# A hybrid decoder step: first loads of the merge issued during the attention, scores weighed in the projection's tail, gates stored by ACT

## The reference

```
h = rmsnorm(x)
qA kA vA | qB kB vB | gate_a gate_b = h @ w_in               # 46 tiles of 128 columns
branch A (8 heads x 64), stick-breaking attention; samples read a paged cache of K and V:
    z = q.k / sqrt(64) + b_h
    a = exp(log_sigmoid(z) + sum over later keys of log_sigmoid(-z));   oA = a @ v
branch B (3 groups x 4 heads x 64), sliding windows (128,1) (512,4) (2048,16) with ALiBi:
    the 3 groups' outputs are mixed by their softmax denominators -> oB
x = x + (sigmoid(gate_a) * (oA @ w_br_a) + sigmoid(gate_b) * (oB @ w_br_b)) @ w_o
x = x + moe(rmsnorm(x))     # top 1 of 4 groups, then top 2 of 8 experts; 32 experts, hidden 512
y = rmsnorm(x)
outputs also: new K and V of the prompt, and the sample caches of branch B shifted by one row
```

## Time and profile before

| what | value |
|---|---|
| median of 3 runs | 1505.83 us (1504.05 to 1510.8) |
| the profiled execution's own time, and its span | 1503.77 us, 1501.9 us |
| PE busy in the span | 1195.9 us, 80% |
| DVE, ACT, POOL busy | 583.7, 248.9, 276.1 us |
| moved by DMA | 455.45 MB, mean 303 GB/s |
| `weigh_a` block | 396 to 421 us |
| `attend` block | 421 to 684 us |
| first `wa` load issued, first `wa` matmul | 684.07 us, 694.43 us |

### The profile page before, as it was taken

One profiled execution on the slowest core, in us unless ns is written; L12 is line 12 of the kernel. 1 busy time (PEld: TensorE's weight loads), 2 busy tenths in 40 slices (PEclk: granted clock), 3 DMA queues, 4 the chain that ended last, 5 costly groups with the idle time before them and its releaser, 6 DMA issues. The chain is left out here.

```text
span 1501.9 us, 14581 instructions
## 1 busy us (share of the span) xinstructions
PE 1195.9 (80%) x5502; PEld 687.0 (46%) x5502; DVE 583.7 (39%) x761; ACT 248.9 (17%) x400; POOL 276.1 (18%) x205
## 2 busy tenths in 40 slices
PE   4999999889469999896379983698888878877870
PEld 3878888678324454444244543233233323323320
DVE  2199999993344444532232225111111111111115
ACT  2121011100234433430000210111101011010112
POOL 2045444542002322220000000111001000100010
PEclk9999999989769999997679995799999999998995
DMA  6789999998137888987912106599999999999964
GB/s 205 294 317 386 390 372 394 399 377 293 43 101 292 316 362 322 381 326 292 314 38 84 43 25 270 195 406 411 405 408 406 408 403 409 408 397 406 410 238 185
DMA packets 102756, 455.45 MB, mean 303 GB/s; under 512 B 13581, under 2 KB 45629, under 8 KB 55365
## 3 DMA queue, kind: packets, MB, share of 16 engines
q1 hardware_dynamic: 71477, 304.12, 51.8%
q0 software_dynamic: 24176, 144.13, 24.7%
q10 hardware_dynamic: 7056, 6.57, 1.4%
HBM read 442.10 MB, written 65.44 MB: 338 GB/s over the span
## 5 line engine op out<-in xcount | busy, mean ns | idle before, releaser
L457 PE MATMUL proj_ps<-hT,w_slots 128*128 128x260 f32 x1472 | 334.8, 388 | 14.2 <-ACT stage L480 12.0
L457 PEld LDWEIGHTS proj_ps<-hT,w_slots 128*128 128x128 f32 x1472 | 281.4, 193 | 65.5 <-issue 21.0
L1759 PE MATMUL ex_gp<-raw,ex_xT 128*64 128x512 f32 x1024 | 232.5, 602 | 21.8 <-DMA raw<-in_w_up_e 14.0
L1773 PE MATMUL ex_yp<-raw,ex_hmT 128*64 128x512 f32 x512 | 141.2, 702 | 66.6 <-DMA raw<-in_w_down_e 66.1
L209 POOL DMA_INDIRECT ring<-in_cache_k_a,run_sb x64 | 137.5, 2149 | 194.5 <-DVE scores L515 167.5
L508 DVE TENSOR_TENSOR ring<-ring,q_rep 128x2048 f32<-128x2048 f32 x64 | 145.9, 2281 | 42.8 <-ACT q_rep L499 41.9
L515 DVE TENSOR_REDUCE scores<-ring 128x32 f32<-128x2048 f32 x64 | 145.8, 2279 | 0.0
L1759 PEld LDWEIGHTS ex_gp<-raw,ex_xT 128*64 128x64 f32 x1024 | 71.2, 138 | 159.3 <-issue 124.4
L1714 DVE TENSOR_TENSOR ex_hm<-ex_sg,ex_gp 64x512 f32<-64x512 f32 x32 | 21.7, 679 | 268.5 <-ACT ex_sg L1694 268.5
L209 POOL DMA_INDIRECT ring<-in_cache_v_a,run_sb x64 | 73.2, 1144 | 258.3 <-PE at_vp L726 242.5
L1773 PEld LDWEIGHTS ex_yp<-raw,ex_hmT 128*64 128x64 f32 x512 | 43.3, 159 | 163.0 <-issue 119.0
(11 more groups left out here) (249 smaller groups left out, 1061.2 us busy)
## 6 DMA issues: line engine op xcount, KB each, us to landing
raw<-in_w_gate_e SPq DMA_DIRECT2D x64, 1024.0 KB, 22.4
raw<-in_w_up_e SPq DMA_DIRECT2D x64, 1024.0 KB, 27.3
raw<-in_w_down_e SPq DMA_DIRECT2D x64, 1024.0 KB, 25.1
o_kvs<-in_cache_kv_b SPq DMA_DIRECT2D x39, 1024.0 KB
w_slots<-in_w_in SPq DMA_DIRECT2D x23, 1024.0 KB, 10.6
mg_kv<-in_cache_kv_b ACTq DMA_DIRECT2D x48, 128.0 KB, 4.9
gate_rows<-stage SPq DMA_DIRECT2D x16, 260.0 KB, 9.7
mg_gate<-gate_rows SPq DMA_DIRECT2D x2, 2080.0 KB, 21.4
```

The costliest lines, as they stand in the source:

```text
L457: last = pe.matmul(pp[:, j, half, 0:H], w[:, m % 2, c, j * P:(j + 1) * P], k.hT[:, c, half * H:(half + 1) * H], start=(c == 0), stop=(c == ...
L1759: last = pe.matmul(gp[at:at + SLOT, j], xT[:, c, :], raw[:, slot, c1 * FF:(c1 + 1) * FF], start=(c == 0), stop=(c == KC - 1))
L1773: last = pe.matmul(yp[h * SLOT:(h + 1) * SLOT, j], hmT[:, c, :], raw[:, slot, o:o + 512], start=(c == 0), stop=(c == FC - 1))
```

## The change

The steps `weigh_a` and its block go away. Its DVE instructions now stand behind the last `reduce` in `project`, its two ACT instructions behind the copy of tile 41, and its two matmuls (`later_keys`) ahead of tile 45. `tables_b` is loaded at the start of `attend`. The gate stores go from SP's stream to ACT's, each right behind the copy that it stores. Some of the merge's loads are issued by SP during the attention, into memory that is no longer read: the keys of samples 0 to 3 (12 transfers) into the queries and keys of branch B's first two head slots, `wa` into branch A's queries and keys, `wb` into `k.scores`, and the gates of tiles 0 to 2 into the last two ring slots. At the start of the merge SP loads the gates of tiles 3 to 7, and ACT loads the keys of samples 4 to 7. For this the lifetimes of several buffers are longer, and x takes the place of `v_rows`.

```diff
+GATES_FIRST = 2
+EARLY_TILES = 3
+def wa_of(k):
+    return k.qk[:, 0:2 * WA // P, :].rearrange("p c n -> p (c n)")[:, 0:WA // P * D].rearrange("p (c n) -> p c n", n=D)
+def wb_of(k):
+    return k.scores[:].rearrange("p b h n -> p (b h n)").rearrange("p (c n) -> p c n", n=D)
+def load_gates(k, sp, part):
+    for what in range(2):
+        a, b = ((0, EARLY_TILES), (EARLY_TILES, KC))[part]
+        sp.dma_start(gate_of(k, a, b)[:, :, what], k.io["gates"].rearrange("p (k c) n -> p k c n", k=2)[:, what, a:b])\
+            .then_inc(k.gates_in[part], 16)
+def load_samples_b(k, eng, what, samples, sem):
+    for b in samples:
+        for g, (_, d) in enumerate(GROUPS):
+            eng.dma_start(kv_b(k, b, g), k.io[f"cache_kv_b{g}"][0, b].rearrange(
+                "(n d) k h e -> n d k (h e)", d=d)[:, 0, what, :]).then_inc(sem, 16)
 def project(k):
...
-                    if m >= 17:
-                        for t in (2 * m - 4, 2 * m - 3):
-                            gates(t)
-                for t in range(N - 4, N):
-                    gates(t)
...
+                def later_keys():
+                    pe.wait_ge(s["rep_laid"], DEC)
+                    pe.wait_ge(s["totals"], 1)
+                    pe.matmul(rp[:], k.const("later"), run[:, :, ROWS_K - 1], start=True, stop=False)
+                    pe.matmul(rp[:], k.const("ones"), rest.rearrange("p a g -> p (a g)"), start=False,
+                              stop=True).then_inc(s["later"], 1)
...
+                    if t == N - 1:
+                        later_keys()
...
+                    if kind[t] == "gate":
+                        act.wait_ge(s["kept"], t + 1)
+                        act.dma_start(io["gates"][:, t - TILES, :], stage[:, t % 2, :]).then_inc(gate_out[t % 2], 16)
...
+                    if t == N - 5:
+                        act.wait_ge(s["clamped"], 1)
+                        act.activation(wt, wt, ACT.Exp).then_inc(s["exped"], 1)
+                        act.wait_ge(s["exped"], 1)
+                        act.activation(wt, wt, ACT.Ln, bias=k.const("ones")[:, 0:1]).then_inc(s["logged"], 1)
+                for j in range(2):
+                    act.wait_ge(gate_out[j], 16 * (GATE_TILES // 2))
...
 def attend(k):
             def _(sp):
+                sp.dma_start(k.tables_b[:], k.io["consts"][:, k.at["rel"][0]:k.at["row_bias"][0]])\
+                    .then_inc(tables_in, 16)
                 for b in range(DEC):
                     if b:
                         used_all(sp, b - 1)
                     shift(k, sp, shift_pieces()[IN_PROJECT + 2 * b:IN_PROJECT + 2 * b + 2])
+                    if b == 5:
+                        sp.wait_ge(s["b_scored"], NG * sum(slot < 2 for slot, _ in UNITS))
+                        load_samples_b(k, sp, 0, range(0, DEC // 2), k.keys_in[0])
+                sp.wait_ge(s["scored"], HA)
+                sp.dma_start(wa_of(k), k.io["w_br_a"][0].rearrange("(c p) n -> p c n", p=P)).then_inc(k.wa_in, 16)
+                sp.wait_ge(s["w_laid"], DEC)
+                sp.dma_start(wb_of(k), k.io["w_br_b"][0].rearrange("(c p) n -> p c n", p=P)).then_inc(k.wb_in, 16)
+                for n in range(RING - GATES_FIRST, RING):
+                    sp.wait_ge(k.ring_used[n], len(range(n, 2 * N_GROUPS, RING)))
+                load_gates(k, sp, 0)
+                sp.wait_ge(tables_in, 16)
...
 def merge(k):
+                load_gates(k, sp, 1)
...
-                load_kv(act, 0, s["keys_in"])
+                load_samples_b(k, act, 0, range(DEC // 2, DEC), k.keys_in[1])
...
-                    if t % QUARTER == 0:
-                        dve.wait_ge(gates_in[t // QUARTER], 16)
+                    if t in (0, EARLY_TILES):
+                        dve.wait_ge(k.gates_in[t // EARLY_TILES], 32)
...
-                    if b == 0:
-                        dve.wait_ge(s["keys_in"], 16 * DEC * NG)
+                    if b % (DEC // 2) == 0:
+                        dve.wait_ge(k.keys_in[b // (DEC // 2)], 16 * DEC // 2 * NG)
```

More of the change, by code:

```diff
@@ L358, in project @@
         rp = k.ps("rep_ps", [P, 512], ctx)
-        s = {n: k.sem("proj_" + n, ctx) for n in ("made", "kept", "turned", "laid", "rep", "rep_laid")}
+        flat = qrep[:].rearrange("p b n -> p (b n)")
+        wt, run = flat[:, 0:A * PAGES], flat[:, A * PAGES:].rearrange("p (a r) -> p a r", r=ROWS_K)
+        flat = k.oT[:].rearrange("p c n -> p (c n)")
+        goes_on = flat[:, 0:A * PAGES].rearrange("p (a r) -> p a r", r=ROWS_K)
+        other, rest = (flat[:, A * PAGES + n * A * GROUPS_K:A * PAGES + (n + 1) * A * GROUPS_K].rearrange(
+            "p (a g) -> p a g", g=GROUPS_K) for n in range(2))
+        s = {n: k.sem("proj_" + n, ctx) for n in (
+            "made", "kept", "turned", "laid", "rep", "rep_laid", "clamped", "exped", "logged", "totals", "later")}
+        own = k.sem("proj_dve", ctx)
         k_out = k.sem("k_out", ctx)
@@ L523, in _ @@
                 reduce(N_GROUPS - 1)
[L526 to L555 removed]
+                for j in range(RING):
+                    dve.wait_ge(k.ring_used[j], len(range(j, N_GROUPS, RING)))
                 link = Chain(dve, own)
+                z = k.scores[:].rearrange("p b h n -> p (b h n)")
+                by_run = lambda ap: ap.rearrange("p (a r) -> p a r", r=ROWS_K)
                 bias = k.b_sb[:].unsqueeze(2).to_broadcast([P, HA, PAGES])
@@ L1217, in _ @@
                 act.wait_ge(s["scores"], 1)
-                load_kv(act, 1, s["values_in"])
+                load_samples_b(k, act, 1, range(DEC), s["values_in"])
                 norm(0)
```

179 lines of the change are left out of this document (70 added, 109 removed).

## The result

The changed kernel takes 1462.76 us (median of 4 runs, 1458.22 to 1466.34) where the kernel before took 1506.11 (4 runs) beside it: a ratio of 0.9706, 95% interval 0.9665 to 0.9747. It is faster, by 43 us. The forecast was 1450 with a range of 1438 to 1467: the direction and the range hold, the forecast is 12.8 us too low. The profiled execution took 1465.87 us, its span is 1464.1.

What follows compares the result with a forecast made beforehand. DMA was taken to bound the second half (`experts`), and waits the dips ahead of it. From the profiled 1503.77 us, -9.2 - 22.9 - 27.1 + 4 gave 1448.6, put at 1450 us (range 1438 to 1467).

Steps and rivals of the forecast that it cites:

- Gate stores: Projection: ACT issuing each gate store behind its copy removes PE's 11.62 us wait; gain 9.2 us (5 to 11.6).
- what is late next: Projection: load 18 of `w_in`, issued about 295.5, lands between 308.6 and 311.3; PE waits 2.4 us.
- Weighing: Between projection and attention: DVE's chain hides behind PE's last tiles; of 28.06 us, gain 22.9 us (20 to 24).
- Early loads in the merge: Merge: PE's wait for `wa` (9.9 us) and DVE's for keys (17.20 us) go; gain 27.1 us (24 to 30).
- Early loads in the attention: Attention: keys cost 1 us, `wa` and `wb` beside the last V loads 3; cost 4 us (0 to 11).
- Early loads paid in full: Attention: all 4.6 MB delay awaited V loads, 11 us in place of 4; 1457 us (up to 1466); chance 0.18.
- The wait moves on in the merge: Merge: second half of keys or gates comes late, giving back 17.2 us; about 1467 us; chance 0.06.
- Slower, by late stores on ACT: Projection: ACT's stores land so late, 21 us, that ACT paces it; from 1506 us on; chance 0.02.

Runs made afterwards that it cites:

- weighing behind the last tile: Changed kernel with `later_keys`, ACT's exp and log and DVE's weighing chain started only after the last tile; 1485.32 us, ratio 0.9819.
- one wait for all keys: Changed kernel, early keys kept, with DVE waiting for both key halves ahead of `scores(0)`; 1470.59 us, ratio 0.9728.
- `wa`, `wb` behind the last V: Changed kernel with SP waiting for the last V group to land before issuing `wa`, `wb` and the first gates; 1455.01 us, ratio 0.9657.
- The old projection's other profile: Kernel before, with only the merge's keys counted on two semaphores and waited for in halves; 1495.56 us, ratio 0.9888.
- all loads in the merge: Changed kernel with `wa`, `wb`, all gates and all 24 key loads issued in the merge, keys still awaited in halves; 1463.38 us, ratio 0.9674.
- last shift in the merge: Changed kernel with output stores behind the last `w_in` load and the two h = 7 shift pieces issued in the merge; 1452.55 us, ratio 0.9598.
- both: Changed kernel with output stores last, small ones off the weighing's semaphore, and `wa`, `wb`, first gates after the last V group; 1447.78 us, ratio 0.9561.
- both with all keys in the merge: Changed kernel with late output stores, early loads held until the last V group landed, and ACT loading all keys in the merge; 1455.41 us, ratio 0.9622.
- stores one load later: Changed kernel with the sample rows' output stores moved behind load 18 of `w_in`, ahead of load 19; 1465.51 us, ratio 0.9699.

## Why the forecast held, and where it was off

The time lies 4 us inside the upper end of the range. The two largest terms came out as forecast; of the other two, one was worth next to nothing and one cost more than twice its size.

**Gate stores: wrong, +0.3 in place of -9.2.** The last tile ended at 393.03 before and at 395.98 after, of which `later_keys` is 2.66 (388.81 - 386.15). 2.2 us of the loss are the earlier wait for `w_in`, which ends before the first of these stores is issued. The first half of the step is right: the stores land after 6.3 us in the median, and ACT waits for none. The step that failed is what is late next. It took load 18 to go out at 295.5 and to land between 308.6 and 311.3, for a wait of 2.4 us. PE ended tile 33 at 296.9 (321.18 - 10.02 less two tiles, 14.29), and SP could issue the load only then, since the slot comes free with that tile; the rest of the small stores cost another 2.3 us. From there two tiles, 14.29 us, are all the cover that a load has, and this one took 22.0: 2.3 + 22.0 - 14.3 is the wait of 10.0. I had carried over the landing of 15.8, less 2.7 us for the two gate stores that no longer stand ahead. But on ACT's queue they travel beside it, and in this trace the share they take is SP's: 15.8 us times 48.0 / 36.9 is 20.6, near the 22.0 measured. Two more kernels with the same projection agree: the load landed after 21.0 us (*weighing behind the last tile*) and 21.6 (*one wait for all keys*), with SP's share at 38 and 36%. A third does not: in *`wa`, `wb` behind the last V* ACT's stores took 11.2%, but POOL had only 44.2% and SP kept 48.9, and the load landed after 17.5 us (its queues from 303 to 320 us follow). The old projection's other profile has 17.6 without any store on ACT. So the landing went with SP's share, but whether ACT's stores take from that share differs between executions.

```profile
q1 hardware_dynamic: 2230, 2.96, 48.9%
q0 software_dynamic: 436, 3.17, 44.2%
q10 hardware_dynamic: 387, 0.74, 11.2%
```

With the stores on SP again the attention starts at about the same time: one wait of 11 us took the place of another. The place of the output stores is the other part: with them last, three profiles have 3.0 to 5.4 us of waits for `w_slots`, but the fourth, with the late keys, has 11.6, so their place does not settle it in every execution. What makes that differ between equal projections was not isolated.

The Trainium skill, page "DMA: Bandwidth & Descriptors", section "Issuing engines are not separate DMA queues", says that transfers of SP, ACT and POOL share the 16 engines, and that issuing on several saves only the time it takes to issue. The trace of the changed kernel agrees here: what the move freed in issuing, the load lost in landing. In the attention, where the prediction used the rule for its 11 us, the size agrees by luck, 11.9 us, but not the way, as the point on the early loads shows.

**Weighing: right, -22.2 in place of -22.9.** 28.06 us between PE's last tile and the attention became 3.25, and `later_keys` took 2.66 in place of 1.9. The run with the weighing behind the last tile gives 18.3 us of it back.

**Early loads in the merge: the size right, -27.8 in place of -27.1; the reason half right.** The 9.9 us for `wa` are shown by the run with all loads in the merge: 10.0 us more to `replicate(1)`. The 17.2 us for the keys are there as well, but moving the loads is not needed for them. Half the keys early with one wait leaves 1.18 us. No key early with two waits leaves 2.44 us in the kernel before, none behind PE's wait for `wa`, and 3.30 where `wa` is early. My step put it all down to the early loads, and treated the hunk that splits the wait as a part of them. At `scores(0)` either does most of the work alone. What the two kernels with `wa` early and late keys lose further on, some 5.5 us, more than half of them at a low granted clock, is a price that the changed kernel with its early keys and two waits doesn't pay; its cause is open.

**Early loads in the attention: mis-sized, +11.9 in place of +4.** The waits themselves were nearly as forecast: 3.6 us more than before (4.14 - 0.56), where I took 3. (At two thirds of the rate V would by my own numbers have lasted until 675.6, a slip of 0.3 us and not of 1.) What I left out is the clock. Behind the wait PE ran at 0.50 to the end of the stage, which cost 5.9 us by the comparison with the run that holds `wa` and `wb` back. The other kernels that issue `wa` beside the last V loads have a wait of 2.83 to 2.86 us at the same place, but in five of the six the clock was back up sooner: from the `at_mp` group to the merge's first matmul they take 14.0 to 14.2 us, where the changed kernel takes 16.2 and the run that holds `wa` back 11.2. There the clock cost 3 to 4 us. The last stretch keeps the two kinds apart without an overlap: 22.2 to 25.7 us in the seven kernels that issue `wa` beside the last V loads, 15.7 to 16.5 in the six that don't. So the early `wa`, `wb` and gates cost 6 to 10 us. The remaining 2.4 us of the 11.9 lie ahead of the last stretch. They can't be put down to the keys, for which I took 1: the kernel before, with its keys in halves and nothing loaded early, is later by more at the same point (250.4 us into the attention, in place of 247.0 before and 249.3 after). And twice a kernel with the early keys and one without them are equal there to 0.1 us: the pair at 242.65 above, and the last shift in the merge and all loads in the merge, both at 248.33.

**The rivals.** *Early loads paid in full* was priced at 1457, up to 1466, and comes closest, but by its size alone: the waits for V are 4.14 us and not 11, and most of the missing time is the gate stores' term and the clock. I spoke against it with a tenth or two of DMA to spare, read off slices of 37 us (slice 12, at 3 tenths, doesn't fit even that); where the last V loads run, the shares of the earlier trace rows already added up to 102%. *The wait moves on in the merge* did not come: DVE waits there for no DMA. *Slower, by late stores on ACT* did not come either: their median landing is 6.3 us, where the forecast needed 21 (20 by its own formula). The chances that I gave add up to 0.99.

**What is left open.** The waits for `w_slots` range from 3.0 to 15.1 us over the profiles with the gate stores on ACT, also between kernels with the same projection. The medians of single kernels carry that with them, so a few us between two of them mean little by themselves. Three kernels stand below the changed one by their intervals: both, the last shift in the merge (its interval ends at 0.9646), and, by a hair, both with all keys in the merge (0.9662 against 0.9665).

## What to carry to other kernels

Loading a stage's data early is worth no more than the waits it removes less those that it makes: issue it once the last transfer that somebody waits for has landed, not as soon as its memory is free. Before moving loads, look whether one wait counts transfers that are wanted later; splitting the wait may give most of the gain, as it did here for the keys. And a store moved to another engine's queue leaves the line of one queue but not the DMA engines: cost what it may take from the transfer that is wanted next.

## What the runs showed of the hardware

- A wait of 2.83 us on PE was followed by 18 us at a granted clock of 0.50, with PE busy 8.88 of 9 us in the first half of them. With a wait of 0.96 us the same 16 matmuls of `at_mp` took 2.00 us in place of 3.68. After a wait of the same length (2.84 us) in *one wait for all keys*, the granted clock was 0.66 in the mean from 656 to 665 us, where the changed kernel has 0.50: how long the low clock lasts is not the same each time.
- A store of 16 KB took SP 8.42 us to issue at 288 us, in the middle of a loaded queue, and the next one 0.32 us. With the stores last, the same two took 0.60 and 0.31 us at 360 us:

```profile
360.36 0.60 SPq L460 DMA_DIRECT2D o_kas<-samp  x1
361.01 0.31 SPq L461 DMA_DIRECT2D o_vas<-samp  x1
```

- The same 1 MB load of `w_in` landed after 22.0, 17.5, 14.8 and 15.8 us (the changed kernel, `wa` and `wb` behind the last V, stores one load later, the kernel before).
